# Sixteen instead of eight k-tiles of a down projection by Strassen's scheme, in five of eight groups

## The reference, cut to what matters

```python
def conv_ffn(h, w_up, conv_w, conv_b, w_down):
    u = h @ w_up
    u = lax.conv_general_dilated(u, conv_w, window_strides=(1,), padding=[(CONV_WIDTH - 1, 0)],
                                 dimension_numbers=('NWC', 'WIO', 'NWC'),
                                 feature_group_count=2 * D_FF) + conv_b
    a, b = jnp.split(u, 2, axis=-1)
    return (jax.nn.gelu(a, approximate=False) * b) @ w_down

def reference(x, ...):
    for i in range(DEPTH):
        ...
        h = rmsnorm(x, norm2_g[i])
        x = x + conv_ffn(h, ffn_w_up[i], ffn_conv_w[i], ffn_conv_b[i], ffn_w_down[i])
    return x
```

## Time and profile before

| | us |
|---|---|
| median of three runs | 1248.47 (1248.42 to 1248.50) |
| profiled execution | 1248.51 |
| its span, first to last instruction | 1246.7 |
| TensorE busy | 1240.8 (6623 matmuls) |
| VectorE busy | 886.5 |
| ScalarE busy | 529.7 |
| GpSimd busy | 193.4 |
| DMA | 120.6 MB, 97 GB/s on average |

### The profile page before, as it was taken

The page is one execution under the profiler, slowest core; times in us unless marked ns, Lnnn a source line. Parts: engine busy times, 40 slices in busy tenths (PEclk is TensorE's granted clock), DMA queues, the critical chain, the costliest instruction groups (busy, mean ns, idle before and its releaser), DMA issues.

```text
span 1246.7 us, 17440 instructions
## 1 busy us (share of the span) xinstructions
PE 1240.8 (100%) x6623; PEld 1061.9 (85%) x6623; DVE 886.5 (71%) x1170; ACT 529.7 (42%) x752; POOL 193.4 (16%) x154
## 2 busy tenths in 40 slices
PE   9999999999999999999999999999999999999999
PEld 8777888888888888898898898898888888888887
DVE  6876586676667566887778777878786677667544
ACT  6654443444444333354254254345453444444221
POOL 3751400112000001403202202202000121000000
PEclk9999999999999999999999999999999999999999
DMA  7212232222221333412222223112332322222232
GB/s 248 69 34 73 98 110 101 100 81 91 99 93 64 98 120 120 164 45 110 69 102 110 67 75 136 68 68 102 106 106 101 101 96 81 91 93 67 111 114 90
DMA packets 20891, 120.62 MB, mean 97 GB/s; under 512 B 2564, under 2 KB 3848, under 8 KB 9064
## 3 DMA queue, kind: packets, MB, share of 16 engines
q1 hardware_dynamic: 19896, 117.61, 27.3%
q10 hardware_dynamic: 720, 1.97, 0.4%
q0 software_dynamic: 224, 0.35, 0.1%
HBM read 117.81 MB, written 2.11 MB: 96 GB/s over the span
## 4 chain that ended last, share of the span: by engine, by line
PE 94%; DVE 3%; DMA 1%; ACT 1%; POOL 1%; issue 1%; DVEq 0%; ACTq 0%; SPq 0%; POOLq 0%
PE ps L1830 21%; PE ps L1831 21%; PE ps L1832 21%; PE ps L2188 4%; PE ps L2192 4%; PE ps L2190 4%; PE ps L2125 4%; PE ps L2127 4%; PE ps L2126 4%; PE ps L2234 2%; PE ps L2236 2%; PE ps L2235 2%; PE ps L1883 1%; PE ps L1980 1%; PE ps L1967 1%; PE ps L1958 1%
## 5 line engine op out<-in xcount | busy, mean ns | idle before, releaser
L1830 PE MATMUL ps<-h_hi,w_hi 128*128 128x512 f32 x832 | 324.7, 390 | 0.0
L1831 PE MATMUL ps<-h_lo,w_hi 128*128 128x512 f32 x832 | 323.8, 389 | 0.0
L1832 PE MATMUL ps<-h_hi,w_lo 128*128 128x512 f32 x832 | 323.7, 389 | 0.0
L880 DVE TENSOR_TENSOR w_lo<-raw,w_hi 128x2048 fp32r<-128x2048 f32 (+1 forms) x107 | 246.8, 2306 | 80.1 <-ACT w_hi L450 80.0
L450 ACT ACTIVATE w_hi<-raw 128x2048 fp32r<-128x2048 f32 (+1 forms) x107 | 200.9, 1877 | 161.6 <-PE ps L2192 84.6
L1832 PEld LDWEIGHTS ps<-h_hi,w_lo 128*128 128x128 f32 x832 | 156.2, 188 | 32.7
L1830 PEld LDWEIGHTS ps<-h_hi,w_hi 128*128 128x128 f32 x832 | 156.2, 188 | 32.5
L1831 PEld LDWEIGHTS ps<-h_lo,w_hi 128*128 128x128 f32 x832 | 156.2, 188 | 31.7
L640 ACT ACTIVATE y<-u,cvec 128x512 f32<-128x512 f32 x88 | 71.2, 816 | 143.8 <-DVE u L1154 76.4
L2188 PE MATMUL ps<-g_hi,w_hi 128*128 128x512 f32 x224 | 87.2, 389 | 0.0
L2190 PE MATMUL ps<-g_lo,w_hi 128*128 128x512 f32 x224 | 87.2, 389 | 0.0
(11 more groups left out here) (274 smaller groups left out, 2527.0 us busy)
## 6 DMA issues: line engine op xcount, KB each, us to landing
raw<-in_w_up SPq DMA_DIRECT2D x44, 1024.0 KB, 4.8
raw<-in_w_ret SPq DMA_DIRECT2D x32, 1024.0 KB, 5.0
raw<-in_w_dn SPq DMA_DIRECT2D x16, 896.0 KB, 4.5
raw<-in_w_dn SPq DMA_DIRECT2D x8, 1024.0 KB, 6.8
raw<-in_w_ao SPq DMA_DIRECT2D x4, 1024.0 KB, 4.9
raw<-in_w_q SPq DMA_DIRECT2D x3, 1024.0 KB, 5.7
gain_x<-in_xT SPq DMA_DIRECT2D x7, 256.0 KB, 4.8
out<-gain_x SPq DMA_DIRECT2D x7, 256.0 KB, 7.4
```

The costliest lines, as they stand in the source:

```text
L880: nc.vector.tensor_tensor(w_lo[:, s, 0:cols], raw[:, s, 0:cols], w_hi[:, s, 0:cols].bitcast(F32), ALU.subtract).then_inc(w_lo_ok, 1)
L1830: nc.tensor.matmul(dst, st[0], mv[0], start=start, stop=False)
L1831: nc.tensor.matmul(dst, st[0], mv[1], start=False, stop=False)
L1832: return nc.tensor.matmul(dst, st[1], mv[0], start=False, stop=stop)
```

## The change

- `DOUBLE` marks five of the eight groups: j = 1 and 2 of layer 0, and j = 1, 2 and 3 of layer 1. Their `down_double` multiplies only KR = 6 k-tiles directly, from one unit of 1536 columns, and the 16 others by two Strassen blocks, a and b, of one unit of 2048 columns each: 14 products, 168 matmuls of 256 columns. Products of b use the same PSUM areas as those of a, so x gets fewer separate additions per block.
- The tokens' sums of the second block (of `g[8:16]`) are formed by GpSimd in eight further steps at the end of `token_sums`. They lie in `h_sum`, which is the memory of `h_lo`, so all but the first wait until the last matmul of the up stage has read h (`w_used`). ScalarE (`next_hi`) and VectorE (`next_lo`) split them into h_hi and h_lo, which hold them through the doubled groups.
- Since h_hi and h_lo are taken, layer 0's tiles of the retention's norm come later: ScalarE makes those of tiles 0 to 5 in group 3, and VectorE all eight `lo_static` after the last subtraction of group 3.
- The loads of a unit wait for the middle splits of the block that held the slot (`load_after_blocks`).

```diff
+KR = FT - 4 * KB
+RW = 2 * KR * P
+DOUBLE = ((False, True, True, False), (False, True, True, True))
...
+        hs = ExitStack()
+        sb("hs_h", [P, KT, S], scope=hs)
+        h_sum = sb("h_sum", [P, KT, S], scope=hs)
+        hs.close()
         h_hi = sb("h_hi", [P, KT, S], F32R)
         h_lo = sb("h_lo", [P, KT, S], F32R)
...
@@ SyncE
                 for j in range(DN_GROUPS):
+                    n = BLOCKS[down_group(layer, j)]
                     for i in range(3):
                         pair, s = down_unit(layer, j, i)
...
+                        if j > 0 and i == 1:
+                            load_after_blocks(unit, s, cols, n)
+                        elif j > 0 and i == 0 and DOUBLE[layer][j - 1]:
+                            load_after_blocks(unit, s, cols, n - 1)
                         else:
+                            load(unit, pair, s, cols)
+
+            def load_after_blocks(src, s, cols, n):
+                sp.wait_ge(dml_ok, 3 * n)
+                sp.dma_start(raw[:, s, 0:cols], src).then_inc(w_loaded[s], 16)
...
@@ ScalarE
+                def next_hi(f):
+                    act.wait_ge(ns_ok, 4 * layer + {T1: 1, T3: 3, T2: 4, T4: 4}[f])
+                    nc.scalar.activation(next_form(f)[0], next_sum(f), ACT.Copy,
+                                         scale=-1.0 if f == T2 else 1.0).then_inc(nhi_ok, 1)
...
                     else:
-                        if not last_layer:
-                            next_operand(2 * j - 2)
-                            next_operand(2 * j - 1)
                         split(*down_unit(layer, j, 1), AW)
+                        act.wait_ge(xe_ok, XE_DN0 + 2 * j)
+                        for m in range(2 * j):
+                            next_operand(m)
...
+                def down_double(j):
+                    g = down_group(layer, j)
+                    n, done = BLOCKS[g], PRODUCTS[g]
+                    (pair_a, a), (pair_b, b) = down_unit(layer, j, 1), down_unit(layer, j, 2)
+                    act.wait_ge(ds_ok, 4 * n + 1)
+                    split(pair_a, a, UW)
+                    act.wait_ge(ds_ok, 4 * (n + 1) + 1)
+                    split(pair_b, b, UW)
+                    for i in range(3):
+                        down_mid_hi(n, a, i, done + i + 1)
+                    down_mid_hi(n + 1, b, 0, done + 5)
+                    split_following(j)
+                    down_mid_hi(n + 1, b, 1, done + 9)
+                    down_mid_hi(n + 1, b, 2, done + 9)
...
@@ VectorE, down
+                    if j == 0:
+                        next_lo(0, T1)
...
-                    if not last_layer:
-                        lo_static(NORM_R, 2 * j)
-                        lo_static(NORM_R, 2 * j + 1)
+                    if not last_layer and j == DN_GROUPS - 1:
+                        for m in range(KT):
+                            lo_static(NORM_R, m)
+
+                def down_double(j):
...
+                    block_first(n, pair_a, a)
+                    split(pair_a, a, UW)
+                    if j == 1:
+                        next_lo(1, T3)
+                        next_lo(2, T4)
+                        next_lo(3, T2)
+                    block_others(n, pair_a, a)
+                    block_first(n + 1, pair_b, b)
+                    split(pair_b, b, UW)
+                    block_others(n + 1, pair_b, b)
+                    down_mid_lo(n, a, 0)
+
+                    dve.wait_ge(dp_done, done + 5)
+                    add_part(x1[:, left], bank + 2, left, dx_ok)
...
@@ GpSimd, end of token_sums
+                base = 2 * KB
+                b12 = next_sum(T2)
+                t1, t3, t4 = (next_sum(f) for f in (T1, T3, T4))
+                ready(base + 2 * KB)
+                pool.wait_ge(fs_ok, 4 * layer + 4)
+                step(tt(b11, part(g_hi, 0, base), part(g_lo, 0, base), ALU.add))
+                pool.wait_ge(w_used, 2 * PAIR_DN[layer])
+                step(tt(b12, part(g_hi, 1, base), part(g_lo, 1, base), ALU.add))
+                tt(t1, b11, b12, ALU.subtract).then_inc(ns_ok, 1)
+                step(tt(t3, part(g_hi, 1, base + KB), b12, ALU.subtract))
+                tt(t3, t3, part(g_lo, 1, base + KB), ALU.add).then_inc(ns_ok, 1)
+                pool.wait_ge(ns_ok, 4 * layer + 2)
+                tt(b12, b11, t3, ALU.add).then_inc(ns_ok, 1)
+                pool.wait_ge(ns_ok, 4 * layer + 3)
+                step(tt(t4, part(g_hi, 0, base + KB), b12, ALU.subtract))
+                tt(t4, t4, part(g_lo, 0, base + KB), ALU.add).then_inc(ns_ok, 1)
...
@@ TensorE
+                def down_double(j):
...
+                    for e in range(2):
+                        for k in range(KR):
...
+                    unit(pair_a, a)
+                    product(both, a, 0, gated(0, 0), True).then_inc(dp_done, 1)
+                    product(c11, a, 1, gated(0, KB), False).then_inc(dp_done, 1)
+                    product(two, a, 2, formed(T1), True).then_inc(dp_done, 1)
+                    product(c21, a, 3, formed(T4), False).then_inc(dp_done, 1)
+                    unit(pair_b, b)
+                    product(both, b, 0, gated(0, 2 * KB), False).then_inc(dp_done, 1)
+                    if j == 1:
+                        pe.wait_ge(nlo_ok, 4 * (layer + 1))
+                    product(two, b, 2, next_formed(T1), False).then_inc(dp_done, 1)
+                    pe.wait_ge(dml_ok, 3 * n + 1)
+                    pe.wait_ge(dx_ok, 5 * g + 1)
+                    product(both, a, 0, formed(T2), False).then_inc(dp_done, 1)
...
```

More of the change, by code:

```diff
@@ L59 @@
 AW = KD * P
+KR = FT - 4 * KB
+RW = 2 * KR * P
 DN_GROUPS = KT // 2
 DN_PAIRS = 3 * DN_GROUPS // 2
+DOUBLE = ((False, True, True, False), (False, True, True, True))
+BLOCKS = [0]
+PRODUCTS = [0]
+for _double in DOUBLE[0] + DOUBLE[1]:
+    BLOCKS.append(BLOCKS[-1] + (2 if _double else 1))
+    PRODUCTS.append(PRODUCTS[-1] + (12 if _double else 6))
 GAINS = 4 * KT
@@ L280, in down_form, with down_cols, next_blocks, next_form @@
             return td_hi[:, i, :, :], td_lo[:, i, :, :]
+        def down_cols(layer, j, i):
+            if DOUBLE[layer][j]:
+                return UW if i else RW
+            return UW if i == 2 else AW
+        def next_blocks(src, f):
+            i = {T1: 0, T3: 1, T4: 2, T2: 3}[f]
+            return src[:, 2 * i:2 * i + 2, :].rearrange("p k (a s) -> p (k a) s", s=HALF)
+        def next_form(f):
+            return next_blocks(h_hi, f), next_blocks(h_lo, f)
+        def next_sum(f):
+            return next_blocks(h_sum, f)
         def down_sum(f):
@@ L1207, in down @@
                 def down(j):
-                    n = down_group(layer, j)
+                    g = down_group(layer, j)
+                    n, done = BLOCKS[g], PRODUCTS[g]
                     bank = 0 if j % 2 else 4
@@ L1225, in down @@
[L1225 to L1231 removed]
+                    block_others(n, pair, s)
@@ L1263, in mlp @@
                 for j in range(DN_GROUPS):
-                    down(j)
+                    (down_double if DOUBLE[layer][j] else down)(j)
                 if not last_layer:
@@ L2175, in down @@
                 def down(j):
-                    n = down_group(layer, j)
+                    g = down_group(layer, j)
+                    n = BLOCKS[g]
                     bank = 0 if j % 2 else 4
@@ L2209, in down @@
                     pe.wait_ge(dml_ok, 3 * n + 3)
-                    pe.wait_ge(dx_ok, 5 * n + 4)
+                    pe.wait_ge(dx_ok, 5 * g + 4)
                     product(both, s, 2, formed(T3), False).then_inc(w_used, 1)
                 for j in range(DN_GROUPS):
-                    down(j)
+                    (down_double if DOUBLE[layer][j] else down)(j)
             mlp(0)
@@ L2474 @@
         wd_arr = np.zeros((DN_GROUPS, 3, P, UW), np.float32)
-        wd_arr[:, 0:2, :, 0:AW] = wd[2 * KB:].transpose(2, 3, 1, 0, 4).reshape(DN_GROUPS, 2, P, AW)
-        wd_arr[:, 2] = wd[:2 * KB].transpose(2, 1, 3, 0, 4).reshape(DN_GROUPS, P, UW)
+        for j in range(DN_GROUPS):
+            two = wd[:, :, j]
+            if DOUBLE[layer][j]:
+                wd_arr[j, 0, :, 0:RW] = two[4 * KB:].transpose(1, 2, 0, 3).reshape(P, RW)
+                wd_arr[j, 1] = two[:2 * KB].transpose(1, 2, 0, 3).reshape(P, UW)
+                wd_arr[j, 2] = two[2 * KB:4 * KB].transpose(1, 2, 0, 3).reshape(P, UW)
+            else:
+                wd_arr[j, 0:2, :, 0:AW] = two[2 * KB:].transpose(2, 1, 0, 3).reshape(2, P, AW)
+                wd_arr[j, 2] = two[:2 * KB].transpose(1, 2, 0, 3).reshape(P, UW)
         wd_arr = wd_arr.reshape(3 * DN_GROUPS, P, UW)
```

168 lines of the change are left out of this document (128 added, 40 removed).

## The result

| | median us | runs |
|---|---|---|
| before | 1248.45 | 1248.42 to 1248.50 (4) |
| after | 1287.31 | 1285.60 to 1289.12 (4) |

The ratio is 1.031, with a 95% interval of 1.0297 to 1.0322: the change costs 38.9 us, where the forecast said 42.7 (1291, range 1272 to 1302). The profiled execution of after is the one of 1285.60 us, with a span of 1283.5, against 1248.51 and 1246.7. What follows accounts for the 36.8 us between the two spans.

The account below looks back on a forecast made before the run. TensorE's gapless row of matmuls was taken to bound the kernel (busy 1240.8 of 1246.7 us). From 1248.5, -4.0 + 26.9 + 12.0 + 4.0 + 3.8 = +42.7 gave 1291 us, range 1272 to 1302.

Parts of the forecast that it names:

- The matmuls: Down projection: five doubled groups take 28.31 us each instead of 29.11 and give back 4.0 us in all.
- The second set of token sums: Up-to-down turn: GpSimd sums and VectorE take turns, TensorE idles 13.1 us, 13.4 per layer with small waits, 26.9 both.
- The 0.3 for unit 2's split: Group 0, behind the 13.1 us idle: unit 2's split ready at 412.6, TensorE arriving at 412.4, 0.3 us of waiting.
- The doubled groups: Down projection: TensorE waits for unit b, 3.7 us in each j = 1 and 1.1 in the others; 12.0 us with extras.
- 10.7 + 0.7 + 0.5: Doubled groups: 10.7 us of waits for b, 5 x 0.14 for a later add, 0.5 in layer 0's j = 2.
- the 0.14 per group: Doubled groups: 0.14 us in each of five for the add that now comes after the middle split.
- The tail of layer 0: Retention's start: all eight h_lo steps follow the last subtraction, so TensorE idles 2.9 and 1.0 us; 4.0 us.
- The clock: Idling lowers TensorE's clock: 1.1 us per layer after group 0's wait, 0.8 after each 3.7 us idle; 3.8 in all.
- (1): Up-to-down turn: VectorE fits two instructions into a gap, so four turns instead of seven precede g_lo: 1277 us; 10%.
- (2): Up-to-down turn: only GpSimd is held up, so the 26.9 and 2.2 of clock fall away: 1262 us; 8%.
- (3): After each long idle the clock stays low some 10 us, +3.5 per layer or more: 1298 to 1301 us; 10%.
- (4): VectorE goes first, GpSimd's steps fit its idle moments, a lands early; only the 4.0 us gain stands: 1244.5 us; 3%.

Follow-up runs that it names:

- b's first sum early: The changed kernel with VectorE making unit b's first sum right behind unit a's split, ahead of the forms and a's other sums: 1280.43 us, ratio 1.0252.
- the clock kept up: The changed kernel with 92 matmuls of 256 columns, result unread, ahead of TensorE's wait for the last g_lo in group 0: 1286.14 us, ratio 1.0298.

## Why the prediction was right, and where its terms were off

**The matmuls, -4.0.** Right. In the last groups of layer 1, which waited for nothing in the version with b's first sum early, a doubled group takes 8.19 + 20.15 us, 0.8 less than 29.14.

**The second set of token sums, 26.9.** The mechanism is the one that the forecast named: the two engines take turns, an instruction each, from the first y step on, up to the seventh sum. Undoing it gave back 28.4 us, doing it alone cost 29.6, and both with the clock in them. TensorE's idling was 12.4 instead of 13.1, since a turn took 2.78 us on average (from GpSimd's start at 382.19 to that at 393.30 there are four), where the forecast had 2.86 (whole instructions, 2.40 + 0.74, would have been 3.14), and TensorE went on 0.05 us after g_lo, where it had 0.2. The 0.3 for unit 2's split was 0, because TensorE's slow stretch after the wait covered it; with the clock kept up it was there, 0.30.

**The doubled groups, 12.0.** Right in kind and 5 us too large: 6.9. (Its parts, 10.7 + 0.7 + 0.5, make 11.9, and nothing is seen of the 0.14 per group: with b's first sum early, j = 2 stays within 0.01 us of its matmuls.) The term that was mis-sized is the time at which unit a is ready: "With a ready just in time, TensorE idles 1.1 us in each doubled group", and 3.7 in j = 1. In layer 0 the middle splits ended at 418.71, not 419.5, and unit a's first sum stood at 423.79, right behind VectorE's own queue, so its load had come within 5.1 us; a was split at 428.76, where the forecast had 430.1. TensorE then waited 2.2 us for b, and in the groups that follow, a was early enough to leave 0.25 in layer 0's j = 2, 1.32 and 0.21 in layer 1's j = 2 and 3. That the chain of sums and splits between a and b was the cause was shown by changing only its order, but for 1.6 us in layer 1's j = 1, where a's own load was late.

**The tail of layer 0, 4.0.** Its two waits were 2.8 and 0.8 when it was tried alone. In the profiled run of after this place cost 6.1; the 2.5 above 3.6 are the slow clock behind the first wait.

**The clock, 3.8.** Too small in group 0 (2.0 and 1.8 instead of 1.1: the matmuls behind the wait stayed slow for 4.0 and 3.6 us, and the wait that was to cover part of it was smaller), too large in j = 1 (there it did not fall in after), and not on the list at the tail, where it took 2.5. In sum 3.8 + 2.5 where 3.8 was forecast. That group 0 alone makes the forecast's 3.8 is chance.

So the profiled run has +36.7 where the forecast had +42.7: the doubled groups 5.1 less, the sums 2.1 less, the tail's waits 0.4 less, the start 0.9 less, the clock 2.5 more. The total is nearer than its terms partly by luck: the clock's 2.5 went the other way than the rest.

**The rivals.** (1), more than one VectorE operation per turn, falls: seven GpSimd steps stood ahead of g_lo. (2), only GpSimd held up, falls by the y steps' 2.5 to 2.9 us. (3), a clock low for longer after the idling, did not come: matmuls were slow for 4.0 and 3.6 us, and for 6.0 at most in any kernel here. (4), faster, was out of reach in this place; it came, in a small way, only where the sums had been moved and the number of groups cut.

## What to carry over

When a step is moved to an idle engine, look at what the busy engine beside it reads in that stretch: seven "free" GpSimd sums took 12.4 us from a VectorE chain with a margin of 1.05 us, and the same sums made TensorE wait for nothing where VectorE's split stood 5.0 us ahead of its use, with 7.0 and 4.6 us of VectorE's idling before and behind it. The time that work takes is not the time it can spare: a margin is read from the end of the work to the consumer's start, and nowhere else. And a wait that stands far ahead of the first use of what it waits for can cost as much as a small gain is worth: the decay table's cost between 0 and 1.3 us, and a doubled group gives 0.8.
